# Choosing the ring slot of each weight slab by the order in which slots come free, and a new placement of the context steps in a routed expert kernel

## The reference, cut to what matters

```python
# block 1, its last part: 64 experts, 8 for each token, one shared expert
hg = einsum('cd,edf->cef', xc, w_eg); hu = einsum('cd,edf->cef', xc, w_eu)
a = silu(hg) * hu * gate[..., None]
routed = einsum('cef,efd->cd', a, w_ed)          # w_eg, w_eu 1024 x 256, w_ed 256 x 1024, for each of 64 experts
x = x + gate2 * (routed + (silu(t @ w_sg) * (t @ w_su)) @ w_sd)
# block 2, layer 0, for x and, independently of x, for the context
u, v, g_a, x_b, g_b = split(h @ w_in)
y_a = u * (spatial_w @ layer_norm(v) + b) * silu(g_a)
y_b = real(fft2(x_b)) * silu(g_b)
ctx = ctx + gate_c * (concat(y_a, y_b) @ w_out)
```

## Time and profile before

| | us |
|---|---|
| median of 3 runs (lowest, highest) | 1112.36 (1111.21, 1112.68) |
| the profiled execution | 1111.33 |
| its span, first to last instruction | 1109.5 |
| TensorE busy, share of the span | 1057.4, 95% |
| VectorE, ScalarE, GpSimd busy | 391.1, 273.1, 52.8 |
| mean DMA rate over the span | 302 GB/s |

### The profile page before, as it was taken

How to read it: one execution, slowest core, us unless ns; L and a number is a source line. 1 busy time by engine, 2 the same in 40 slices (tenths; PEclk the granted TensorE clock), 3 DMA queues, 4 the chain that set the end, 5 groups by cost and what they waited for, 6 DMA issues and landing times.

```text
span 1109.5 us, 15876 instructions
## 1 busy us (share of the span) xinstructions
PE 1057.4 (95%) x6286; PEld 725.3 (65%) x6286; DVE 391.1 (35%) x1021; ACT 273.1 (25%) x615; POOL 52.8 (5%) x85
## 2 busy tenths in 40 slices
PE   6999999999999899898999989989989999999998
PEld 4786776688766365465555556446448888887567
DVE  1398966522532222111121222121333011433851
ACT  2124134511511111111211111111322101213951
POOL 0000202013100000000000000001000001100001
PEclk9999989999999999999999999999999999999999
DMA  9999387964679999999999999999997434100200
GB/s 385 349 420 421 123 338 280 420 259 156 248 280 365 420 421 420 421 419 421 421 421 420 421 421 421 421 420 418 415 415 294 139 123 152 39 1 1 114 1 38
DMA packets 48554, 335.11 MB, mean 302 GB/s; under 512 B 5440, under 2 KB 6816, under 8 KB 8672
## 3 DMA queue, kind: packets, MB, share of 16 engines
q1 hardware_dynamic: 46080, 329.01, 73.1%
q10 hardware_dynamic: 2176, 3.37, 1.1%
q0 software_dynamic: 224, 1.70, 0.4%
HBM read 333.02 MB, written 1.05 MB: 301 GB/s over the span
## 4 chain that ended last, share of the span: by engine, by line
PE 83%; DMA 11%; DVE 4%; issue 1%; ACT 1%; SPq 0%; DVEq 0%; ACTq 0%
PE bank L1100 12%; PE bank L544 12%; DMA ring<-experts 10%; PE bank L1143 6%; PE bank L1055 5%; PE bank L1240 5%; PE bank L942 3%; PE bank L461 3%; PE bank L999 3%; PE bank L1328 3%; PE bank L836 2%; PE bank L964 2%; PE bank L1283 2%; PE bank L851 2%; PE bank L674 2%; PE bank L610 2%
## 5 line engine op out<-in xcount | busy, mean ns | idle before, releaser
L1100 PE MATMUL bank<-ring,arena 128*32 128x512 f32 (+1 forms) x1120 | 175.8, 602 | 13.8 <-DMA ring<-experts 12.5
L544 PE MATMUL bank<-hT,ring 128*128 128x256 f32 x608 | 134.3, 381 | 1.1 <-ACT hT L1522 1.1
L1100 PEld LDWEIGHTS bank<-ring,arena 128*32 128x32 f32 (+1 forms) x1120 | 52.4, 120 | 118.5 <-issue 118.2
L544 PEld LDWEIGHTS bank<-hT,ring 128*128 128x128 f32 x608 | 114.6, 190 | 22.1 <-issue 6.9
L1143 PE MATMUL bank<-ring,conds 128*32 128x512 f32 (+1 forms) x560 | 90.9, 622 | 11.5 <-DMA ring<-experts 9.7
L1143 PEld LDWEIGHTS bank<-ring,conds 128*32 128x32 f32 (+1 forms) x560 | 27.1, 123 | 57.5 <-issue 53.3
L2334 DVE TENSOR_TENSOR yhalf<-bank,yhalf 128x512 fp32r<-128x512 f32 x48 | 33.2, 692 | 89.0 <-ACT yhalf L1720 89.0
L2319 DVE SCALAR_TENSOR_TENSOR conds<-bank,gcol,conds 128x256 f32<-128x256 f32 x24 | 11.6, 484 | 141.3 <-ACT conds L1712 130.1
L1459 POOL TENSOR_TENSOR hT<-hT 128x256 f32<-128x256 f32 x30 | 21.7, 725 | 825.7 <-ACT hT L1516 824.2
L942 PE MATMUL bank<-picked,halves 128*128 128x256 f32 x384 | 58.1, 294 | 0.5 <-DVE arena L2232 0.3
L1240 PE MATMUL bank<-hT,ring 128*128 128x256 f32 x256 | 57.0, 379 | 0.0
(11 more groups left out here) (402 smaller groups left out, 1440.4 us busy)
## 6 DMA issues: line engine op xcount, KB each, us to landing
ring<-experts SPq DMA_DIRECT2D x188, 1024.0 KB, 15.2
ring<-stream SPq DMA_DIRECT2D x119, 1024.0 KB, 12.5
ring<-experts SPq DMA_DIRECT2D x8, 512.0 KB, 9.4
arena<-consts POOLq DMA_DIRECT2D x1, 1408.0 KB, 11.9
resid<-x SPq DMA_DIRECT2D x1, 1024.0 KB, 5.1
resid<-ctx ACTq DMA_DIRECT2D x1, 1024.0 KB, 10.0
arena<-stream SPq DMA_DIRECT2D x1, 1024.0 KB, 9.7
bias_room<-rpb ACTq DMA_DIRECT2D x2, 438.0 KB, 5.8
```

The source lines that it names most:

```text
L544: mm = mmul(o[:, 0:n_tok], w[:, k, t * P:(t + 1) * P], hT[:, k, 0:n_tok], start=(k == 0), stop=(k == KT - 1))
L1100: mm = mmul(o[at:at + n_slots, :], xg_of(m, kk)[:, at:at + n_slots], w[g][:, k, :], start=(kk == 0), stop=(kk == KT - 1))
```

## The change

A slab no longer goes to slot `n % RING`. `new_slab` gives it the slot of the slab whose end stands first in TensorE's program among those whose slots haven't been handed out again. Up to the first expert slab the old round holds; from there on the list `given` is kept in TensorE's order. SyncE waits for the end of that slab (`room_of[n]`). The order in which slabs are asked for is still TensorE's. All places that worked out a slot by `n % RING` read `slot_of[n]` instead. The table `CONTEXT` is new: the same steps, at other units. A slab may now stay in use over several units (that of z12 and z13 from unit 9 to unit 11).

```diff
-CONTEXT = """0: z4 |
-1: z5 | z0 z1 fa0
-2: fb0 fa1 |
-3: | fb1
-4: z2 z3 z6 | z7
-5: | fa2
-6: | fb2
-7: fa3 | fb3 v0
-8: v1 |
-9: v2 v3 |
-10: shd0 | z8 z9
-11: z12 z13 | sp0
-13: sp1 z10 z11 | z14 z15
-14: sp2 |
-15: sp3 fold0 | o0 o1
-16: o2 o3 |
-20: o4 o5 | o6 o7 squares0
-21: | sum0
+CONTEXT = """1: z4 z5 |
+2: z0 z1 fa0 | fb0 fa1
+3: fb1 z2 |
+4: z3 z6 z7 | fa2
+5: | fb2
+6: fa3 | fb3 v0
+8: v1 | v2 v3
+9: shd0 z8 | z9 z12
+11: z13 |
+12: sp0 sp1 z10 z11 z14 |
+13: | z15 sp2
+14: | sp3 fold0 o0
+15: | o1 o2
+16: o3 |
+18: o4 | o5
+19: o6 |
+20: | o7
+21: squares0 | sum0
 22: norm0 | norm1"""
...
+        slot_of = []
+        room_of = []
+        let_go = []
+        given = []
+        spare = []
+
+        def new_slab(src):
+
+            n = len(slabs)
+            if src[0] == "exp" and not given:
+                given.append(list(m for m in let_go if m >= n - RING))
+            old = given[0].pop(0) if given else n - RING
+            slabs.append(src)
+            slab_end.append(None)
+            room_of.append(old if n >= RING else None)
+            slot_of.append(slot_of[old] if n >= RING else n)
+            loads.append(sum(slot_of[m] == slot_of[n] for m in range(n + 1)))
+            return n
+
+        def ends(n, end):
+
+            slab_end[n] = end
+            let_go.append(n)
+            if given:
+                given[0].append(n)
...
             def arrived(n):
 
-                pe.wait_ge(slab_in[n % RING], 16 * loads[n])
-                return ring[:, n % RING, :]
+                pe.wait_ge(slab_in[slot_of[n]], 16 * loads[n])
+                return ring[:, slot_of[n], :]
...
                         for n in ns:
-                            slab_end[n] = ("gu_half", m + 1)
+                            ends(n, ("gu_half", m + 1))
...
             def load(n):
 
-                slot = n % RING
+                slot, old = slot_of[n], room_of[n]
...
-                    if n >= RING:
-                        given_back(slab_end[n - RING])
+                    if old is not None:
+                        given_back(slab_end[old])
                     sp.dma_start(room, w).then_inc(slab_in[slot], 16)
```

More of the change, by code:

```diff
@@ L430, in ask @@
             def ask(src):
[L432 to L436, removed]
+                return new_slab(src)
             def arrived(n):
-                pe.wait_ge(slab_in[n % RING], 16 * loads[n])
-                return ring[:, n % RING, :]
+                pe.wait_ge(slab_in[slot_of[n]], 16 * loads[n])
+                return ring[:, slot_of[n], :]
             def take_slab(src):
@@ L469, in ada_slab @@
                             mm.then_inc(S("ada_read"), 1)
-                            slab_end[n] = ("ada_read", ada_reads[0])
+                            ends(n, ("ada_read", ada_reads[0]))
             ada_reads = [0]
             def leave_to_vector(i):
[L476 to L479, removed]
+                n = new_slab(("ada1", SIDE[i]))
+                ends(n, ("ada_side", i + 1))
                 side_slabs.append(n)
@@ L561, in tok_tiles @@
                     close_group(mm, name)
-                slab_end[n] = name
+                ends(n, name)
             def pair_of_heads(kind):
@@ L677, in first_inputs @@
                     if t == 1:
-                        slab_end[in_at[slab]] = name
+                        ends(in_at[slab], name)
             def head_squares(j):
@@ L724, in _ @@
                 head_squares(2 * t + 1)
-            slab_end[n] = ("qk3", 1)
+            ends(n, ("qk3", 1))
             _, n = take_slab(("in", 4))
@@ L751, in _ @@
             close_group(mm, "krot4")
-            slab_end[n] = "krot4"
+            ends(n, "krot4")
             leave_to_vector(8)
@@ L782, in _ @@
                 close_group(mm, ("uq", g))
-            slab_end[n] = ("uq", 3)
+            ends(n, ("uq", 3))
             pe.wait_ge(S("kvn"), 1)
@@ L924, in _ @@
             shu_part(1, 5, range(KT))
-            slab_end[nu] = ("shu", 1)
+            ends(nu, ("shu", 1))
             pe.wait_ge(S("gates_made"), 1)
@@ L982, in second_halves @@
                     if halved(slabs[n]):
-                        before = sum(halved(slabs[i]) for i in range(n % RING, n, RING))
+                        before = sum(halved(slabs[i]) and slot_of[i] == slot_of[n] for i in range(n))
                         pe.wait_ge(second_in(n), 16 * before + 16)
@@ L1001, in oabc @@
                 if d % 2:
-                    slab_end[n] = ("oabc", d)
+                    ends(n, ("oabc", d))
             def channels(o, folds, n):
@@ L1076, in context_step @@
                 if kind in ("z", "v") and i % 2 and (kind, i) != ("z", 1):
-                    slab_end[held[kind]] = (kind + "c", i)
+                    ends(held[kind], (kind + "c", i))
             def context_steps(m, half):
@@ L1145, in unit @@
                 for n in ns:
-                    slab_end[n] = ("y", m, 1)
+                    ends(n, ("y", m, 1))
             for m in range(LAST + 1):
@@ L1157, in arrived @@
                     pe.wait_ge(S("more_in"), 192 * m + 192)
-                    return ring[:, (len(slabs) + UN * j + u) % RING, :].rearrange("p (k c) -> p k c", c=512)
+                    return ring[:, slot_of[spare[UN * j + u]], :].rearrange("p (k c) -> p k c", c=512)
                 pe.wait_ge(S("more_on_vector"), 7 * m + 1)
@@ L1231, in _ @@
             context_keys(1, 1)
-            slab_end[ck] = ("k2c", 1)
+            ends(ck, ("k2c", 1))
             for s in range(2):
@@ L1264, in _ @@
                 if i % 2:
-                    slab_end[n] = ("z", i)
+                    ends(n, ("z", i))
                 if 4 <= i < 8:
@@ L1285, in _ @@
                 if d % 2:
-                    slab_end[n] = ("oabx", d)
+                    ends(n, ("oabx", d))
             _, cv = take_slab(("cin", 1))
@@ L1303, in _ @@
                 tok_tile(("v2", t), cv, t, 5 - t)
-            slab_end[cv] = ("v2", 1)
+            ends(cv, ("v2", 1))
             last_attention(*c_pairs)
@@ L1394, in _ @@
             with sp.If(more > 0):
-                for n in range(more0, more0 + 3 * UN):
-                    given_back(slab_end[n - RING])
+                for n in spare:
+                    given_back(slab_end[n])
                 with sp.Fori(0, more) as m:
```

40 lines of the change are left out of this document (21 added, 19 removed).

## The result

| | before, us | after, us |
|---|---|---|
| median of 4 runs each (lowest, highest) | 1112.52 (1111.21, 1115.09) | 1104.19 (1103.81, 1106.77) |
| the profiled execution | 1111.33 | 1103.81 |
| its span | 1109.5 | 1102.0 |
| first gate/up block starts, after the program's start | 316.69 | 314.17 |
| from there to the last down projection (below: **the stage**) | 500.50 | 495.49 |

The ratio of the times is 0.9928, with a 95% interval of 0.9913 to 0.9942: faster by 0.7%, 8.3 us, against 4.4 foretold and a range whose low end was 1106.4. The lower half of the table splits the 7.5 us between the two profiled executions: 5.0 are in the stage, none in the tail, and 2.5 stand ahead of the stage, where the change has no instruction.

A forecast was written before the change was run, and what follows sets the result against it. The transfer stream was taken to bound the expert stage. Gains of 2.5 + 0.4 + 2.0 = 4.9 us, reduced to 4.4, took the median from 1112.4 to 1108.0 us; range 1106.4 to 1110.6.

The forecast's parts named there:

- What bounds the kernel: Expert stage: bound by the 420 GB/s transfer stream until its last slab lands; only an earlier full stream helps.
- Parts 1 and 2: Start of the expert stream: z4 out of unit 0 gains 2.5 + 0.4, earlier slots 2.0; 4.9 us less up to 0.5.
- Part 2: Unit 1: first half's four freed slots go out while z4 and z5 run; gain 2.0 us, also alone with the old table.
- Part 3: Context steps moved to other units: totals stay, no DMA cost if slots return in time; shortest cover about 3 us.
- The rival in which the stream runs dry: Mid-stage: piled steps and held slabs make TensorE late, leaving 1 to 3 us of gain, 1109.4 to 1111.4; chance 0.2.
- the one in which the regained start is worth nothing: Unit 23: TensorE as late as before, so only 1.1 us comes, 1111.3; chance 0.05.
- Part 4: Last unit: TensorE, ahead without the four-tile pile, stalls some 4.5 us; last down projection comes 4.4 to 4.8 us earlier.
- Part 5: Units 20 and 21: GpSimd's squares and additions finish before the sum, 6.5 against 7.1 us, no wait; tail moves with the stage.
- The rival of the clock: Unit 23 to the end: clock stays low after the long wait, making the kernel 7 us slower, 1120; chance 0.05.
- the Sum: Whole kernel: 4.9 us for the stream, less up to 0.5 and what the last unit keeps back, gives 4.4 us.

The follow-up runs named there:

- with filler: Kernel after plus 20 unread 128x128 by 128 matmuls on constants, placed ahead of the stage: median 1108.51 us, ratio 0.9959 to the kernel before, stage 495.60.
- the first units alone: Kernel after with new slots, but new table rows only for units 0 to 2 (fb1 in unit 3): medians 1105.19 and 1106.00 us, ratios 0.9934 and 0.994.

## Why the prediction was right or wrong

**What bounds the kernel** held, with one limit. Fill the stream 5 us earlier, and the stage ends 5 us earlier: 500.5, 501.0 and 500.8 us with the old start and old slots; 498.5 to 499.5 with the new slots and one or two tiles in unit 0; 495.5, 495.6, 495.6, 495.8, 495.8, 496.7 and 497.1 with the new start. The limit: in three of these last seven (495.6 with filler, 496.7 and 497.1) the last down projection waited 0.94 us for DVE and not for a slab, behind 6.8 us of low clock. There TensorE, and not the stream, ends the stage.

**Parts 1 and 2 together** were right: 4.9 less up to 0.5 foretold, 5.0 in the pair of profiles, 4.5 on the mean of four profiles after (496.26) against two before (500.73). On the clock of the kernel before, the issue foretold at 324.2 came at 324.0 (7.35 behind the start), the four from 334.3 at 334.2.

**Part 2's sentence "with the old table worth 2.0 alone" was too high.** It gave 1.2 to 1.6. The landings behind the start of the stage say why. The transfer of the second pair's neighbour, with its unowned 1.2 us delay in the kernel before, landed without it in this kernel, so the next pair (issued at the same 17.7) was 1.46 us late where it had been 0.42, and the delay came two transfers later, behind a full queue, as an extra 1.38. Such delays of 0.9 to 1.7 us come three or four times among the expert slabs of a profile, and where one falls into a gap that is there anyway it is free. That is 1 us either way for a kernel that still has gaps, and probably also why z4 in unit 0 gave 498.48 with z0, z1 and fa0 in unit 1 and 499.50 with these in unit 2; that no run separates.

**Part 3** held: no step moved elsewhere cost anything. From the start of the stage to the last expert slab, the kernel after has one issue that comes too late for the queue, the common one of 3.1 us at the start; none between 350 and 800 us. The shortest cover behind the refill is 7.7 us from issue to landing, 2.7 over the floor of 5.0 (about 3 were foretold), but it comes early, at 375 us, and not behind units 9 and 13. The longest wait for ACT or DVE inside the stage is the 1.72 us at 787.99, as before. The rival in which the stream runs dry did not come, nor the one in which the regained start is worth nothing.

**Part 4** was close in its numbers: last expert slab landed 496.5 behind the start (813.2 on the clock before, 813 to 814 foretold), last down projection 495.49 (812.2; 812.3 to 813 foretold), stall 5.41 (4 to 5 foretold), block behind it 5.06. (5.3 was foretold; 6.55 and 6.28 came in two other profiles.) Wrong was the part that it gave to the lost pile of four tiles: TensorE was to be ahead in unit 23 because of it, and the kernel with the old pile ended its stage as early (495.60). What brings TensorE forward is the earlier stream itself, which it follows.

**Part 5** held: GpSimd's additions take 5.07 us from 762.33 and end at 767.40; the sum starts at 767.89 without a wait. 0.6 us were foretold between them, 0.5 came. The tail "moves with the stage": 292.3 in both.

```profile
762.33 5.07 POOL L1482 TENSOR_TENSOR hT<-hT 128x256 f32<-128x256 f32 x6 [479.66 <-ACT hT L1539]
...
767.89 0.70 PE L533 MATMUL bank<-hT,ones 128*128 128x256 f32 x2
```

**The rival of the clock** is refuted in its size. After the 5.41 us stall the level fell and was back within the same block:

```profile
800.00:804.00 4.00, 3.34 (x20) 1.04 (x24) 0.00 (x0) 0.00 (x0) 0.00 (x0) 0.57 1.03 410
...
807.00:814.00 7.00, 5.43 (x44) 2.55 (x43) 1.47 (x4) 1.17 (x2) 0.00 (x0) 1.00 1.03 423
```

In 807 to 814 the engine waits between bursts and shows 1.00. In two of the four profiles of the kernel after the low level lasted 6.8 us, and was gone ahead of the last down projection (3.64 us) in these too; 9 us of busy time at the lower level would have been needed for a slower kernel. The rule of the Trainium skill, "TensorE: Matmul & The Clock Gate", section "HAM oscillation — how this bites in real kernels", is about bursts that are shorter than the DMA waits between them, each of which then starts cold. The trace agrees for the one block whose wait was longer than it, 5.41 us ahead of 3.64 us of work. Behind it TensorE is busy 5.43 us of 7, its waits are shorter than that, and the rule isn't put to the test.

**Where it failed is the Sum,** which took the gain of the stage off a time whose other parts it held fixed: "The profiled execution goes from 1111.3 to 1106.9. The median of the runs is 1.0 higher". The measured 1103.8 is under 1106.9 by 3.1: 0.6 for the stage (5.0, not 4.4), 2.5 ahead of it. The step that failed is the term for the time ahead of the stage, which was put at nothing: measured, the first block started 2.52 us earlier. No term stood for the low-clock stretches at 144 and 178 us, though such stretches were in the trace that I read, and the three times given (1111.21, 1112.36, 1112.68) did not show how far they can move a median of four. By all executions seen since, the kernel after is at 1106.5, inside the range by 0.1, 1.5 us under the forecast. The range allowed 1.6 us for everything to that side, and the draws alone are 2.5.

Still open: what decides which draw an execution gets. The profiles give one sign, which no run tests. In the twelve profiles without filler, the sums at 141 us (L828 or L808) start between 140.56 and 141.03 in all seven with the long stretch, and between 141.07 and 141.86 in all five with the short one. So the draw goes with a shift of some tenths of a us that is there well ahead of 144 us, and the 0.50 us by which the first profile after was late at 141 us stands on the good side. Whether a change to the program can move it is open.

Also open is what the whole time gained beyond the 4.5 us of the stage, 1.3 us by the medians and 2.0 by the means. The unequal draws would account for (8/21 - 7/87) x 2.5 = 0.75 us, an estimate. Part may be the group of the kernel before at 1114.4 to 1115.1, 22% of its executions, for which the kernel after has no counterpart. None of that group has been profiled. A low stretch on the last down projection, as with the first units alone, would cost it 1.7 us; in the kernel after, that stretch falls on the block ahead of it, where TensorE had time to spare. That is an argument, and no run here shows it.

## What to carry to other kernels

A stage that is bound by a full transfer stream loses at its end about what the stream loses at its start, so look for the first late issues and ask which block of work must end before each slot comes free. Nothing elective should stand ahead of that block, and a slot should go out in the order of return. Moving one 3.6 us tile by one unit was worth 2.4 to 4.0 us, and the new placement of all later steps nothing that the times show.

Split every difference into the parts ahead of, inside and behind the edited stage before explaining it, and run the unchanged code twice: here a third of the first comparison's gain lay where no edit was, and came and went with the same program. Then count how often each kernel gets the good draw, too: a difference that comes by chance can still come more often in one of them.

## What the runs showed of the hardware that was not expected

The time of one unchanged program falls into groups, and the profiles tie these to stretches of granted clock 0.5 at a few places of the program. At 144 us it came for 3.4 or for 6.8 us, and at 178 us for 3.4 or not at all; the two together are the 2.5 us. Behind the 5.4 to 5.7 us stall in the last unit it came for 3.4 us in two profiles of the kernel after and for 6.8 in two, and from that block's start to the end of the stage these two took 0.5 to 0.9 us more (9.6 and 9.9 against 9.0 and 9.1). The executions between 1106.2 and 1106.8 weren't profiled.

The length of the wait ahead doesn't decide whether the level falls. The last down projection of the kernel before ran at 1.00 behind an idle time of 2.92 us; with the first units alone, the same block behind the same 2.92 us ran at the lower level and took 5.34 us:

```profile
812.00:816.00 4.00, 4.00 (x24) 1.07 (x16) 0.69 (x1) 0.59 (x1) 0.00 (x0) 0.57 1.03 428
```

And a queued slab of 1 MiB lands 2.48 us behind the one before, but three or four times among the 192 expert slabs it is 3.4 to 4.2 us behind it, and no instruction of the program was found that accounts for it. It came once or twice among the first fourteen asked for in the stage, and in every profile once between the 151st and the 160th slab of the list and once between the 221st and the 233rd.
